# Expert biases: from bias products on TensorE to rows loaded to all partitions and added by VectorE

## The chip, the cores and the metric

The kernel runs on one core of a Trainium2 chip. The metric is the device time of one execution in microseconds (us). Five engines work side by side: TensorE (PE in the profile: matmuls; PEld: its weight loads), VectorE (DVE), ScalarE (ACT), GpSimd (POOL) and SyncE (SP), which here issues the loads. Each runs its own instructions in the order written and waits on semaphores. Sixteen DMA engines move the data.

## The reference

One inference step of a one-layer decoder for 512 prompt tokens and 64 sample tokens, model width 1024: two token mixers (gated linear attention and sparse attention), an output projection, and a mixture of experts, 4 of 32 per token. The change concerns the experts only. Each expert's tokens form a block of 128 rows, and for a block `xb` with expert `e` the reference computes

```python
gate = jnp.minimum(xb @ w_gate[e] + b_gate[e], SWIGLU_LIMIT)
up = jnp.clip(xb @ w_up[e] + b_up[e], -SWIGLU_LIMIT, SWIGLU_LIMIT)
return ((up + 1.0) * gate * jax.nn.sigmoid(SWIGLU_ALPHA * gate)) @ w_down[e] + b_down[e]
```

with `SWIGLU_LIMIT` 7 and `SWIGLU_ALPHA` 1.702. All three weight matrices of an expert are 1024 x 1024 in fp32. The rows that come out are weighed and added to their tokens. `b_down` enters elsewhere and isn't touched.

## The kernel before, in words

Seven stages follow each other, with a barrier between them. The last, `experts`, handles 32 blocks (one per expert here) and takes about two thirds of the time. A block needs three products of 128 x 1024 by 1024 x 1024: gate, up and down. Each weight matrix is loaded in four quarters of 1024 KB (two of the eight 128-row slices each), so a block has twelve quarters. `load_quarter` issues one on SyncE into one of six landing slots.

For accuracy in TensorE's faster fp32 form, both operands are split into a rounded high part and a rest. For a quarter, ScalarE writes the high part (`high_part`, L3064), VectorE the rest (`rest_part`, L3152: quarter minus high part). Both go to rings of four slots. TensorE then runs 12 matmuls of 512 columns for the quarter (`product`, L2950) and increments `s_used`. ScalarE may write a slot of the ring when the product four quarters earlier is done; SyncE may reload a landing slot when the rest of the quarter six earlier is written (`s_rest`).

The order of a step on each engine, written out by hand (`step`), for block k and its predecessor `prev`:

- TensorE: gate(k) with 4 quarters, the turn of the activations of k-1 (8 transposes, L2958), up(k), the turn of the input rows of k+1, down(k-1).
- VectorE: rests 4 to 6, `read_gate` (L3165: PSUM to `g`, min with 7), rest 7, the rest of the turned activations (`rest_T`, L3156), rests 8 to 10, `read_up` (L3171: PSUM to `u`, clipped), `activate` (L3176: (u+1)*g, L3179: times the sigmoid), rest 11, the rest of the turned rows (L3156), rests 0 to 3 of the next block.
- ScalarE: high parts 4 to 7, the sigmoid (L3081), the high part of the turned activations (`acts_T`, L3067), high parts 8 to 11, that of the turned rows, high parts 0 to 2, the weighing of the down product (L3095), high part 3.
- SyncE: bias rows of block k (L2831), then the loads of gate, up and down quarters.
- GpSimd: the gather of a block's input rows (L2193) and the scatter that adds a block's output rows in memory (L2911).

The biases enter the sums as products. In the router stage GpSimd splits `b_gate` and `b_up` into three bf16 parts (L2341 to L2344) and stores them (L2346); SyncE waits for that (`s_bp`) before it issues the first weight quarters. In a step SyncE loads, for each of gate and up and each half of 512 columns, three rows of 512 bf16 to partitions 0, 32, 64 and 96 onward (four loads of 3 KB). TensorE begins the sums of gate and up with four matmuls of 3 rows (`start_with_bias`, L2936) with `ones` as the other operand, all four ahead of gate(k).

## Time and profile before

| | us |
|---|---|
| median of 3 runs | 1809.06 |
| their range | 1807.79 to 1809.69 |
| the profiled execution's own time | 1809.45 |
| its span | 1807.3 |

| engine | busy us | share of the span |
|---|---|---|
| TensorE, matmuls | 1691.8 | 94% |
| VectorE | 1424.3 | 79% |
| ScalarE | 1103.0 | 61% |
| GpSimd | 330.7 | 18% |

The span runs from the first to the last instruction. Matmuls are pipelined and their ends modelled, so a busy TensorE is not one at its peak. A releaser ("<-") is what ended an engine's idle time. Shares over the whole span mix stages with different limits, so the rows below are mostly of the expert stage, which begins near 640 us.

### The profile page before, as it was taken

To read this page: it belongs to the slowest core of one execution; us is meant where nothing else is said; L and a number is where in the kernel's file an instruction comes from. 1 tells how busy PE (TensorE), PEld (TensorE's weight loads), DVE (VectorE), ACT (ScalarE), POOL (GpSimd) and SP (SyncE) were. 2 spreads that over 40 slices of the span, in tenths; PEclk is the share of its full clock that TensorE was granted. 3 is DMA by queue.
4 is the path that set the end of the run, shared out by engine and by line. 5 is a ranking of instruction groups with operands and counts; after the bars stand their busy time and mean duration, and the time that the engine had idled before them with its cause. 6 is when DMAs were issued, how large, how long until landed. Compare 5 with 4: busy or idle time off the path is not lost.

```text
span 1807.3 us, 27029 instructions
## 1 busy us (share of the span) xinstructions
PE 1691.8 (94%) x9028; PEld 1311.5 (73%) x9028; DVE 1424.3 (79%) x1356; ACT 1103.0 (61%) x1052; POOL 330.7 (18%) x310
## 2 busy tenths in 40 slices
PE   3999978888998779999999999999999999999996
PEld 2776766555564568888888888888888888888884
DVE  4422563577425879999999999999999999999997
ACT  4222343354334366777777777777777777777773
POOL 0000011300001012122222312222231222223211
PEclk9999999599998779999999999999999999999998
DMA  9454553610226479999999999999999999999993
GB/s 347 174 185 172 98 157 97 223 80 3 69 97 188 173 276 335 379 376 374 369 378 377 372 374 379 377 373 373 379 374 373 387 371 373 384 373 374 385 349 124
DMA packets 114598, 516.08 MB, mean 286 GB/s; under 512 B 25870, under 2 KB 47710, under 8 KB 62058
## 3 DMA queue, kind: packets, MB, share of 16 engines
q1 hardware_dynamic: 101082, 483.48, 70.9%
q0 software_dynamic: 12800, 29.45, 5.8%
q10 hardware_dynamic: 656, 2.36, 0.3%
q8 instruction: 36, 0.59, 0.1%
q14 instruction: 24, 0.20, 0.0%
HBM read 502.75 MB, written 31.09 MB: 295 GB/s over the span
## 4 chain that ended last, share of the span: by engine, by line
PE 61%; DVE 1%; DMA 1%; ACT 0%; issue 0%; SPq 0%; DVEq 0%; POOL 0%; POOLq 0%; ACTq 0%
PE banks L2950 57%; PE banks L2958 3%; PE banks L2936 1%; DMA routing<-in_g_final 0%; DMA ffn_rows<-weighed,block_rows 0%; DVE split L3152 0%; DVE arena L3249 0%; PE banks L3005 0%; ACT split L3064 0%; DVE arena L3242 0%; DVE arena L3241 0%; SPq L2870 0%; DVEq L2816 0%; POOL wait_taken L2888 0%; DVE gates L3165 0%
## 5 line engine op out<-in xcount | busy, mean ns | idle before, releaser
L2950 PE MATMUL banks<-split 128*128 128x512 f32 x4608 | 1076.9, 393 | 1.1 <-DVE split L3152 1.1
L2950 PEld LDWEIGHTS banks<-split 128*128 128x128 f32 x4608 | 861.0, 188 | 186.2 <-issue 7.2
L3152 DVE TENSOR_TENSOR split<-expert_buffers,split 128x2048 fp32r<-128x2048 f32 x384 | 864.8, 2284 | 42.7 <-ACT split L3064 40.5
L3064 ACT ACTIVATE split<-expert_buffers 128x2048 fp32r<-128x2048 f32 x384 | 733.2, 1918 | 217.1 <-PE banks L2950 213.3
L2888 POOL TENSOR_TENSOR wait_taken<-routing 128x1 f32<-128x1 f32 x62 | 76.3, 1231 | 811.7 <-PE banks L2958 464.6
L2911 POOL DMA_INDIRECT ffn_rows<-weighed,block_rows x31 | 107.7, 3473 | 4.8 <-issue 4.8
L662 PE MATMUL banks<-w_in_high,hT_high 128*128 128x476 f32 x192 | 76.0, 396 | 4.4 <-DVE hT_low L498 4.4
L3156 DVE TENSOR_TENSOR split<-banks,split 128x1024 fp32r<-128x1024 f32 x64 | 77.8, 1215 | 0.7 <-ACT split L3067 0.7
L662 PE MATMUL banks<-w_in_high,hT_low 128*128 128x476 f32 x192 | 73.5, 383 | 0.0
L3067 ACT ACTIVATE split<-banks 128x1024 fp32r<-128x1024 f32 x64 | 64.5, 1008 | 6.0 <-PE banks L2958 6.0
L573 DVE COPY arena<-banks 128x476 f32<-128x476 f32 x12 | 7.8, 654 | 70.0 <-PE banks L662 69.9
L662 PE MATMUL banks<-w_in_low,hT_high 128*128 128x476 f32 x160 | 60.5, 378 | 0.0
L1850 ACT ACTIVATE arena<-banks 128x512 f32<-128x512 f32 (+1 forms) x45 | 24.5, 586 | 58.1 <-PE banks L2114 19.3
L1520 ACT ACTIVATE arena<-banks,arena 128x128 f32<-128x128 f32 (+3 forms) x64 | 33.2, 526 | 39.2 <-DVE arena L1562 39.0
L662 PEld LDWEIGHTS banks<-w_in_high,hT_high 128*128 128x128 f32 x192 | 36.8, 192 | 22.0 <-issue 16.8
L3095 ACT ACTIVATE weighed<-banks,block_weights 128x1024 f32<-128x1024 f32 x31 | 34.6, 1117 | 29.3 <-PE banks L2950 29.3
L3081 ACT ACTIVATE sigmoids<-gates 128x1024 f32<-128x1024 f32 x32 | 34.0, 1063 | 26.2 <-DVE gates L3165 26.2
L2893 POOL TENSOR_TENSOR routing<-routing 128x1 int32<-128x1 int32 x31 | 40.6, 1310 | 16.1 <-issue 8.3
L840 POOL MEMSET arena<- 128x2560 f32 x1 | 2.2, 2237 | 214.2 <-POOLq L127 214.2
L662 PEld LDWEIGHTS banks<-w_in_high,hT_low 128*128 128x128 f32 x192 | 36.8, 191 | 5.8
L2958 PEld LDWEIGHTS banks<-routing 128*128 128x128 f32 x256 | 33.9, 192 | 9.1 <-DVE bias_ones L3147 6.7
L3179 DVE TENSOR_TENSOR ups<-ups,sigmoids 128x1024 f32<-128x1024 f32 x32 | 39.3, 1230 | 1.1
(396 smaller groups left out, 1728.5 us busy)
## 6 DMA issues: line engine op xcount, KB each, us to landing
expert_buffers<-in_w_gate SPq DMA_DIRECT2D x128, 1024.0 KB, 8.0
expert_buffers<-in_w_up SPq DMA_DIRECT2D x128, 1024.0 KB, 19.0
expert_buffers<-in_w_down SPq DMA_DIRECT2D x128, 1024.0 KB, 8.6
arena<-in_w_ada SPq DMA_DIRECT2D x16, 1024.0 KB, 4.9
w_in_landing<-in_w_in SPq DMA_DIRECT2D x5, 1904.0 KB, 9.0
arena<-in_w_ada SPq DMA_DIRECT2D x4, 2048.0 KB, 19.9
arena<-in_x_prompt SPq DMA_DIRECT2D x8, 512.0 KB, 9.4
arena<-in_cache_cmp SPq DMA_DIRECT2D x32, 128.0 KB, 2.9
```

What stands on the lines that cost most here:

```text
L662: last = pe.matmul(ps[0:n, 4 + t, 0:CW], h[:, kt, t0:t0 + n].bitcast(F32R), w.bitcast(F32R), start=(kt == 0 and j == 0), stop=(kt == KT - ...
L2888: pool.tensor_tensor(sums[s_sum.index(sem)], one, one, ALU.add).then_inc(sem, 1)
L2893: pool.tensor_tensor(tokens, core.row_of[:, bass.ds(k, 1)], none, ALU.add).then_inc(s_tok, 1)
L2911: pool.indirect_dma_start(core.ffn_d, bass.IndirectOffsetOnAxis(ap=row_out.bitcast(U32), axis=0), y, None, bounds_check=NTOK - 1, oob_is_e ...
L2950: last = pe.matmul(ps[:, bank + c, :], x[:, kt * P:(kt + 1) * P].bitcast(F32R), wt.bitcast(F32R), start=(m == 2 and kt == 0 and x is xs[0] ...
L2958: last = pe.transpose(ps[:, TB + kt // 4, (kt % 4) * P:(kt % 4 + 1) * P], v[:, kt, :], ident)
L3064: act.activation(high[:, j % RING_Q].bitcast(F32R), v, ACT.Copy).then_inc(s_high, 1)
L3067: act.activation(dst.bitcast(F32R), ps[:, TB:TB + 2, :].rearrange("p b n -> p (b n)"), ACT.Copy).then_inc(sem, 1)
L3095: act.activation(y, ps[:, DB:DB + 2, :].rearrange("p b n -> p (b n)"), ACT.Copy, scale=weight_out).then_inc(s_y, 1)
L3152: dve.tensor_tensor(rest[:, j % RING_Q].bitcast(F32R), v, high[:, j % RING_Q], ALU.subtract).then_inc(s_rest, 1)
L3156: dve.tensor_tensor(lo.bitcast(F32R), ps[:, TB:TB + 2, :].rearrange("p b n -> p (b n)"), hi, ALU.subtract).then_inc(out, 1)
L3179: dve.tensor_tensor(u, u, s, ALU.mult).then_inc(s_a, 1)
```

## The change

The bias parts, their store and their waits go from the router stage, and the bias matmuls from TensorE; the first matmul of each sum now starts it. SyncE loads the 4 KB bias row of the expert, once for gate and once for up, to all 128 partitions, straight into `g` and `u`: the gates' once the previous activation is done (`s_a`), between the first and second up quarters, and the ups' once the previous activations are turned (`s_atp`), behind the down quarters. VectorE adds as it reads, so the clipping is done afterwards. For the gates it is folded into the product with the sigmoid (`gated`, placed ahead of rest 10), while ScalarE takes relu(7 - g) first and then a sigmoid of 1.702 * 7 - 1.702 * that, which is the sigmoid of 1.702 * min(g, 7). For the ups it is an instruction of its own.

```diff
@@ router stage
-                    for i, name in enumerate(("b_gate", "b_up")):
-                        sp.dma_start(b32[:, i * BQ:(i + 1) * BQ], io[name][0].rearrange("e (q n) -> (e q) n", n=BQ)).then_inc(s_b, 16)
...
-                    sp.wait_ge(s_bp, 1)
...
-            pool.wait_ge(s_b, 32)
-            for a in range(3):
-                if a < 2:
-                    link(pool.tensor_copy(bparts[:, a, :], b32))
-                    link(pool.tensor_tensor(b32, b32, bparts[:, a, :], ALU.subtract))
-                else:
-                    pool.tensor_copy(bparts[:, a, :], b32).then_inc(s_bp, 1)
-            pool.wait_ge(s_bp, 1)
-            pool.dma_start(core.bias_d.rearrange("e q a m n -> (e q) (a m n)"), bparts.rearrange("p a n -> p (a n)")
-                           ).then_inc(s_bo, 16)
...
@@ experts, SyncE
+            def load_biases(m, e):
+
+                sp.dma_start((g, u)[m], core.io[("b_gate", "b_up")[m]][0][bass.ds(e, 1), :].to_broadcast([P, D])
+                             ).then_inc(s_bias[m], 16)
...
             e = expert(0)
-            biases(0, e, None)
-            biases(1, e, None)
-
             for q in range(2, 4):
                 sp.wait_ge(s_rest, q - 1)
                 load_quarter(core, sp, e, 1, q, q - 2)
+            sp.wait_ge(core.s_begun, 16 * ST)
+            for m in range(2):
+                load_biases(m, e)
 
             def step(k, prev):
 
-                free = 1 if is_zero(prev) else 12 * prev
                 e = expert(k)
-                biases(0, e, free)
-                biases(1, e, free)
                 quarters(0, e, prev, 0)
-                e = expert(k)
-                quarters(1, e, prev, 4)
-                e = expert(prev)
-                quarters(2, e, prev, 8)
+                quarters(1, e, prev, 4, range(1))
+                sp.wait_ge(s_a, k)
+                load_biases(0, e)
+                quarters(1, e, prev, 4, range(1, 4))
+                quarters(2, expert(prev), prev, 8)
+                sp.wait_ge(s_atp, k)
+                load_biases(1, e)
@@ experts, TensorE
-            def start_with_bias(m, n, bank):
-
-                pe.wait_ge(s_bias[m], 32 * n)
-                for c in range(2):
-                    r0 = bias_row(m, c)
-                    pe.matmul(ps[:, bank + c, :], ones[r0:r0 + 3, :], bias[r0:r0 + 3, :], start=True, stop=False)
-
...
-                                             start=(m == 2 and kt == 0 and x is xs[0] and wt is hi[c]),
+                                             start=(kt == 0 and x is xs[0] and wt is hi[c]),
...
-                start_with_bias(0, k + 1, GB)
-                start_with_bias(1, k + 1, UB)
...
@@ experts, ScalarE
                 if is_zero(k):
+                    act.wait_ge(s_seven, 1)
                     act.wait_ge(core.s_begun, 16 * ST)
-                act.activation(s, g, ACT.Sigmoid, scale=ALPHA).then_inc(s_sig, 1)
+                act.activation(s, g, ACT.Relu, scale=-1.0, bias=seven[:, 0:1]).then_inc(s_room, 1)
+                act.wait_ge(s_room, k + 1)
+                act.activation(s, s, ACT.Sigmoid, scale=-ALPHA, bias=seven[:, 1:2]).then_inc(s_sig, 1)
@@ experts, VectorE
-                else:
-                    dve.wait_ge(s_a, k)
-                dve.tensor_scalar(g, ps[:, GB:GB + 2, :].rearrange("p b n -> p (b n)"), LIMIT, None, ALU.min).then_inc(s_g, 1)
+                dve.wait_ge(s_bias[0], 16 * (k + 1))
+                dve.tensor_tensor(g, ps[:, GB:GB + 2, :].rearrange("p b n -> p (b n)"), g, ALU.add).then_inc(s_g, 1)
+
+            def gated(k):
+                dve.wait_ge(s_sig, k + 1)
+                dve.scalar_tensor_tensor(g, g, LIMIT, s, ALU.min, ALU.mult).then_inc(s_part, 1)
 
             def read_up(k, used):
                 dve.wait_ge(s_used, used)
-                if not is_zero(k):
-                    dve.wait_ge(s_atp, k)
-                dve.tensor_scalar(u, ps[:, UB:UB + 2, :].rearrange("p b n -> p (b n)"), -LIMIT, LIMIT, ALU.max, ALU.min
-                                  ).then_inc(s_u, 1)
+                dve.wait_ge(s_bias[1], 16 * (k + 1))
+                dve.tensor_tensor(u, ps[:, UB:UB + 2, :].rearrange("p b n -> p (b n)"), u, ALU.add).then_inc(s_u, 1)
 
             def activate(k):
                 dve.wait_ge(s_u, k + 1)
-                dve.scalar_tensor_tensor(u, u, 1.0, g, ALU.add, ALU.mult).then_inc(s_t, 1)
-                dve.wait_ge(s_t, k + 1)
-                dve.wait_ge(s_sig, k + 1)
-                dve.tensor_tensor(u, u, s, ALU.mult).then_inc(s_a, 1)
+                dve.tensor_scalar(u, u, -LIMIT, LIMIT, ALU.max, ALU.min).then_inc(s_clip, 1)
+                dve.wait_ge(s_clip, k + 1)
+                dve.wait_ge(s_part, k + 1)
+                dve.scalar_tensor_tensor(u, u, 1.0, g, ALU.add, ALU.mult).then_inc(s_a, 1)
...
-                for j in range(8, 11):
+                for j in range(8, 10):
                     rest_part(j, prev)
+                gated(k)
+                rest_part(10, prev)
                 read_up(k, at + 8)
                 activate(k)
                 rest_part(11, prev)
```

## Rows read from the trace of the kernel before

**Rows 1.** Chain that ended last, by line, from the page.
```profile
PE banks L2950 57%; PE banks L2958 3%; PE banks L2936 1%; DMA routing<-in_g_final 0%; DMA ffn_rows<-weighed,block_rows 0%; DVE split L3152 0%; DVE arena L3249 0%; PE banks L3005 0%; ACT split L3064 0%; DVE arena L3242 0%; DVE arena L3241 0%; SPq L2870 0%; DVEq L2816 0%; POOL wait_taken L2888 0%; DVE gates L3165 0%
```
**Rows 2.** Timeline of one step, VectorE and ScalarE (start us, us, instruction, [idle before]).
```profile
1007.35 1.22 DVE L3165 TENSOR_SCALAR gates<-banks 128x1024 f32<-128x1024 f32 x1
1008.48 2.28 DVE L3152 TENSOR_TENSOR split<-expert_buffers,split 128x2048 fp32r<-128x2048 f32 x1
1008.60 1.06 ACT L3081 ACTIVATE sigmoids<-gates 128x1024 f32<-128x1024 f32 x1 [0.77 <-DVE gates L3165]
1009.57 1.01 ACT L3067 ACTIVATE split<-banks 128x1024 fp32r<-128x1024 f32 x1
1010.47 3.75 ACT L3064 ACTIVATE split<-expert_buffers 128x2048 fp32r<-128x2048 f32 x2
1010.68 1.22 DVE L3156 TENSOR_TENSOR split<-banks,split 128x1024 fp32r<-128x1024 f32 x1
1012.40 6.85 DVE L3152 TENSOR_TENSOR split<-expert_buffers,split 128x2048 fp32r<-128x2048 f32 x3 [0.51 <-ACT split L3064]
...
1019.17 1.22 DVE L3171 TENSOR_SCALAR ups<-banks 128x1024 f32<-128x1024 f32 x1
...
1020.43 1.23 DVE L3176 SCALAR_TENSOR_TENSOR ups<-ups,gates 128x1024 f32<-128x1024 f32 x1
...
1021.69 1.23 DVE L3179 TENSOR_TENSOR ups<-ups,sigmoids 128x1024 f32<-128x1024 f32 x1
1022.84 2.28 DVE L3152 TENSOR_TENSOR split<-expert_buffers,split 128x2048 fp32r<-128x2048 f32 x1
...
1025.04 1.21 DVE L3156 TENSOR_TENSOR split<-banks,split 128x1024 fp32r<-128x1024 f32 x1
1026.18 11.08 DVE L3152 TENSOR_TENSOR split<-expert_buffers,split 128x2048 fp32r<-128x2048 f32 x5
...
1037.50 2.29 DVE L3152 TENSOR_TENSOR split<-expert_buffers,split 128x2048 fp32r<-128x2048 f32 x1 [0.24 <-ACT split L3064]
...
1040.23 2.29 DVE L3152 TENSOR_TENSOR split<-expert_buffers,split 128x2048 fp32r<-128x2048 f32 x1 [0.43 <-ACT split L3064]
...
1042.44 1.22 DVE L3165 TENSOR_SCALAR gates<-banks 128x1024 f32<-128x1024 f32 x1
```
**Rows 3.** Windows: length, busy us of each engine, PEclk, DMA share, GB/s.
```profile
1007.35:1042.44 35.09, 35.09 (x166) 28.85 (x165) 33.77 (x20) 26.75 (x17) 9.00 (x7) 1.00 0.98 371
...
970.00:975.00 5.00, 5.00 (x28) 4.25 (x27) 4.95 (x3) 3.42 (x4) 0.00 (x0) 1.00 1.02 347
975.00:980.00 5.00, 5.00 (x24) 4.14 (x23) 4.49 (x4) 4.20 (x4) 0.00 (x0) 1.00 1.01 415
```
**Rows 4.** Table of waits, 700 to 1750 us (total us, times, longest).
```profile
ACT split L3064 <- PE banks L2950: 199.2, 270, 0.8
DVE split L3152 <- ACT split L3064: 35.4, 90, 0.5
```
**Rows 5.** Timeline of TensorE where a step begins.
```profile
1029.41 0.40 PE L2936 MATMUL banks<-block_biases,bias_ones 3*128 3x512 bf16 x4
1029.74 11.22 PE L2950 MATMUL banks<-split 128*128 128x512 f32 x48
```
**Rows 6.** Groups by line and shape, VectorE, an earlier stage.
```profile
L456 DVE TENSOR_SCALAR arena<-arena 128x1024 f32<-128x1024 f32 x4 | 2.9, 746 | 10.0 <-ACT arena L358 10.0
```
**Rows 7.** One scatter (timeline); all scatters, 700 to 1750 us (median us to landing).
```profile
997.97 3.48 POOL L2911 DMA_INDIRECT ffn_rows<-weighed,block_rows  x1 [0.15 <-issue]
...
ffn_rows<-weighed,block_rows POOLq DMA_INDIRECT x30, 13.2
```
**Rows 8.** GpSimd's last bias pass (timeline); first weight loads (one line's instructions).
```profile
578.42 0.95 POOL L2344 CAST arena<-arena 128x512 bf16<-128x512 f32 x1
...
L2727 SPq DMA_DIRECT2D expert_buffers<-in_w_gate x4: 440/560/642, 614.4 to 616.0; - x4
```
**Rows 9.** One line's instructions, the sigmoid (duration ns, first and last start).
```profile
L3081 ACT ACT_TABLE_LOAD  x1: 1283/1283/1283, 658.7 to 658.7; - x1
```

More of the change, by code:

```diff
@@ L2250, in output_and_router @@
     upper = Stack(core, core.z1 + NT * D + ST * 512, ARENA)
-    BQ = D * NE // P
-    b32 = core.arena[:, hole[0]:hole[0] + 2 * BQ]
-    bparts = upper.take(3 * 2 * BQ // 2).bitcast(BF16).rearrange("p (a n) -> p a n", a=3)
     bsplit = core.named("down_bias_split", upper.at, D)[:, 0:D]
@@ L2763, in experts @@
     w, s_w = core.w, core.s_w
-    bias = own("block_biases", 512 // 2).bitcast(BF16)
-    ones = own("bias_ones", P // 2).bitcast(BF16)
+    seven = own("limit", 2)
     xg, tokens, none = core.xg, core.tokens, core.none
@@ L2773, in experts @@
     s_bias = [core.sem(f"bias_in{i}") for i in range(2)]
+    s_seven, s_part, s_room, s_clip = core.sem("limit_ready"), core.sem("gate_times_sigmoid"), core.sem("gate_room"), core.sem("up_clipped")
     s_high, s_rest, s_used = (core.sem(n) for n in ("quarters_rounded", "quarters_split", "quarters_used"))
     s_xg = core.s_xg
[L2776 to L2777 removed]
+    s_rowo, s_xtp, s_xh, s_xt = (core.sem(n) for n in (
+        "weights_taken", "xT_ps", "xT_rounded", "xT_split"))
     s_g, s_u, s_sig, s_a, s_atp, s_ah, s_at = (core.sem(n) for n in (
         "gate_read", "up_read", "sigmoid", "act_ready", "aT_ps", "aT_rounded", "aT_split"))
[L2780 removed]
+    s_y, s_yo = core.sem("down_read"), core.sem("rows_added")
     s_tok = core.sem("tokens_taken")
@@ L2823, in expert, with quarters @@
                 return sp.value_load(blocks[0:1, bass.ds(k, 1)], min_val=0, max_val=NE - 1)
-            def biases(m, e, used):
-                if used is not None:
-                    sp.wait_ge(s_used, used)
-                for c in range(2):
-                    r0 = bias_row(m, c)
-                    sp.dma_start(bias[r0:r0 + 3, :].rearrange("a (q n) -> a q n", q=2),
-                                 core.bias_d[bass.ds(e, 1), 2 * c:2 * c + 2, :, m, :].rearrange("e q a n -> (e a) q n")
-                                 ).then_inc(s_bias[m], 16)
-            def quarters(m, e, prev, c):
-                for q in range(4):
+            def load_biases(m, e):
+                sp.dma_start((g, u)[m], core.io[("b_gate", "b_up")[m]][0][bass.ds(e, 1), :].to_broadcast([P, D])
+                             ).then_inc(s_bias[m], 16)
+            def quarters(m, e, prev, c, some=range(4)):
+                for q in some:
                     sp.wait_ge(s_rest, 12 * prev + c + q + 9 - LANDING)
@@ L3146, in _ @@
         def _(dve):
-            dve.memset(ones, 1.0).then_inc(s_ones, 1)
+            dve.memset(seven[:, 0:1], LIMIT)
+            dve.memset(seven[:, 1:2], LIMIT * ALPHA).then_inc(s_seven, 1)
             def rest_part(j, prev):
```

22 lines of the change are left out of this document (6 added, 16 removed).

## The prediction, made before the result was known

> **What bounds the kernel now.** I read the page's chain of waits first: 57% of the span on it is the matmul line of the expert products, L2950, and the lines of VectorE and ScalarE have 0% each [rows 1]. The span holds 32 blocks of the expert stage, and in it each step is alike, so I read one step closely, from one read of the gates by VectorE (L3165, at 1007.35) to the next (1042.44): a step of 35.09 us [rows 2]. In that window TensorE is busy for all of it at the full clock, VectorE for 33.77 us, ScalarE for 26.75 us, and the DMA engines for a share of 0.98 at 371 GB/s [rows 3]. So three resources stand close together: TensorE sets the pace, VectorE has 1.3 us to spare, the DMA engines next to nothing by their share. The table of waits says how they hang together: ScalarE's rounding (L3064) waits for TensorE 270 times (199.2 us, ring of four slots), VectorE's subtraction (L3152) waits for ScalarE 90 times, 35.4 us in all, or 1.2 us a step [rows 4]. VectorE idles only because it has caught up with the ring. Its idle places are in [rows 2]: 0.51 us before rest 8 (at 1012.40), 0.24 and 0.43 us before rests 5 and 6 (1037.50 and 1040.23). ("Rest n" is the n-th L3152 of the written order of a step.)
>
> How late may VectorE be? Rest 0 of the next block ends at 1026.18 + 2.28 = 1028.46 [rows 2], the product that uses it starts at 1029.74 [rows 5]: 1.3 us. That is the tightest place; I take it as the slack.
>
> **TensorE's part.** Four bias matmuls go. They use rows 0, 32, 64 and 96, start within 0.1 us of each other and the next matmul starts 0.33 us after the first of them [rows 5]. 128 instructions of 384 ns would look like 49 us; they are worth 0.33 us x 32 = 10.6 us at most. TensorE's step would be 35.09 - 0.33 = 34.76 us. The waits on the gate and up reads stay, so the idle before them stays as well; if it went too, 0.3 us more a step would be saved, and if something of the bias time only turns into that idle, nothing. I take 34.76.
>
> **VectorE's part.** The two reads become additions of a PSUM and an SBUF operand. The same kind of instruction of the same size stands in the step: L3156, 1.21 us, against 1.22 us for the read [rows 2]. Nothing changes. Of the two instructions after read_up, one (min and product with the sigmoid) moves ahead of rest 10, one clip is added, one stays. Start to start, now: L3171 to L3176 1.26, L3176 to L3179 1.26, L3179 to rest 11 1.15, together 3.67 us [rows 2]. Then: read_up 1.26, clip, product 1.15. The clip is a one-input instruction from SBUF to SBUF. That kind, 128x1024 f32, took 746 ns [rows 6]; read from PSUM it takes 1.22 us [rows 2]. The source here is SBUF, so I take 0.75 + 0.03 = 0.78 us, and 1.26 as the upper end. Sum 3.19 us, plus 1.15 for the moved one: 4.34, so +0.67 us a step (up to +1.15).
>
> **ScalarE's part, and the detour.** Sigmoid becomes two passes, Relu and Sigmoid, each taken at the 1.06 us of the sigmoid row, and a wait for its own result between them (0.05 us, estimated from the 0.03 to 0.1 us between an end and a dependent start in [rows 2]). ScalarE has time for it on average (26.75 + 1.1 of 35 us). But behind the sigmoid in its fixed order stands the rounding of the turned activations (L3067), and behind that the rounding of quarter 8, and VectorE waits for both. Now: gates read until 1008.57, sigmoid 1008.60, L3067 1009.57, high part 8 from 1010.47 to 1012.39, rest 8 at 1012.40 [rows 2]; that chain is already the one that ends last, as the 0.51 us of idle shows. Rest 7 (to 1010.76) covers only the first part. With one more pass: Relu 1008.60 to 1009.66, sigmoid 1009.71, L3067 from 1010.68, high part 8 from 1011.58 to 1013.50, rest 8 at 1013.52. That is +1.12 us, and no work of VectorE's can fill it, since its order is fixed too. The ends: Relu as cheap as the cheapest pass of 1024 elements in the step, L3067 at 1.01 us, +1.06; with a slow hand-over, +1.25.
>
> **VectorE's step.** Packed, without the idle before rests 5 and 6, the step now is: read_gate to rest 8 5.05, to read_up 6.77, to rest 11 3.67, to rest 0 3.34, seven rests at (11.08 - 2.28) / 4 = 2.20 each 15.4; sum 34.23 us [rows 2]. New: 34.23 + 1.12 + 0.67 = 36.02 us. It begins and ends on VectorE, so slack can't absorb it for long, and it is above TensorE's 34.76. TensorE is then held at rests 11 and 0. The idle before rests 5 and 6 should go, since TensorE is no longer ahead.
>
> Per step 36.02 - 35.09 = +0.93 us. There are 31 steps with this order (blocks 1 to 31; in block 0 the placing of the overflow stands between the read and rest 7 and covers the longer sigmoid): +28.8 us, less the 1.3 us of slack used up once, less 0.3 us of bias matmuls in block 0: +27 us.
>
> **DMA.** A step loads twelve quarters of 1024 KB. The step moved 371 GB/s x 35.09 us = 13.0 MB [rows 3] (the quarters alone are 12.6). Each bias row of 4 KB is now written to 128 partitions: 2 x 128 x 4096 B = 1.05 MB a step; the old 3 KB loads were nothing. At 36.02 us that asks for (13.0 + 1.05) / 36.02 = 390 GB/s. Were these engines at their limit at a share of 0.98, they could give 371 / 0.98 = 379. But at full share they gave 347 in one stretch and 415 in the next of 5 us [rows 3]. The low stretch lies in the time of the adding scatter of the rows: it was issued at 997.97, so at 962.9 in the step before, and takes 13.2 us to land, until 976 [rows 7]. Taking 347 for 13.2 us and 414 for the rest, a step of 14.05 MB needs 13.2 + (14.05 - 4.58) / 0.414 = 36.1 us; by 379 throughout, 37.1 us. So this limit lies right beside VectorE's. As the load of the gates' bias stands in the queue ahead of two weight quarters whose slots were freed late (by rests 11 and 0; the second, freed at 1028.46, is wanted by ScalarE 1.92 us ahead of a rest 6 that, packed, would start 11.0 us later, so within 9.1 us), I add 0.2 us a step, between 0 and 0.5 (1.05 MB take 2.5 us of queue in all): +6 us.
>
> The Trainium skill's page "DMA: Bandwidth & Descriptors" (Specifications) has a limit of ~358 GB/s from HBM for a core; by it a step would take 14.05 / 0.358 = 39.2 us, some 1940 us in all, an estimate by that page of the Trainium skill. The trace already stands above that figure, 371 over a whole step and 415 at the best [rows 3], and the measurement decides; I give this nothing.
>
> **Waits that are added or moved.** SyncE waits for the activation (s_a) before the gates' bias, behind the first up quarter; the next quarter waits for rest 11, which follows the activation on VectorE, so nothing is late. It waits for s_atp before the ups' bias, at the place of the old bias loads, between rests 5 and 6; the next issue waits for rest 6. In the DMA-bound case it can be late. Landing has some 18 us for the gates and 14 for the ups: enough against 13.2 us, the longest landing in the rows [rows 7]. In the router stage GpSimd's five passes, a store, and SyncE's wait for them go. They end at 579.4, the first weight loads go out at 614.4 [rows 8]: nothing, and 1 us either way for what they disturbed.
>
> **Sum.** +27 + 6 = +33 us on the profiled execution's 1809.45 us (span 1807.3), which is 0.4 us above the median of the runs. Predicted: 1842 us.
>
> **Rivals.**
> DMA-bound, slower still: the bias writes don't fit, the six landing slots are all in flight, ScalarE waits for weights. 36.6 (the 36.1 with the waits of a full queue) to 37.4 us a step, 31 x 1.5 to 2.3 = +47 to +71: 1856 to 1880. For it: a share of 0.98 now. Against: no wait of ScalarE for a DMA in the table, and 415 GB/s beside the scatter.
> TensorE-bound, faster: the removed matmuls count and VectorE hides the rest. 31 x -0.33 = -10 us: 1799. It decides if VectorE's packed step stays below 34.76 us. VectorE's busy time alone would allow it (33.77 + 0.67 = 34.44); the detour behind the sigmoid, which already shows as idle, speaks against. If only half of both terms came, the step would be 35.1: no change, 1809.
> Relu and Sigmoid in different tables: two loads a step. The one load in [rows 9] took 1.28 us; both lie on the detour: +2.56 us a step, 79 us more: 1921. In this trace Sigmoid and Copy alternate after one load. "ScalarE: Activation LUTs" (Table sets) of the Trainium skill says that cheap functions such as relu are in every set; no row here has a Relu. I give it 2%.
>
> **How the numbers follow.** Forecast (chain of VectorE and ScalarE, 1834 to 1853): 57%. DMA-bound: 29%. Tables: 2%. TensorE-bound: 5%. No change: 3%. Forecast's mechanism with its lower ends (1825 to 1834): 4%. Range 1830 to 1880. A measurement of this kernel tells a change of about 0.2% (4 us) from none; so faster 5%, same 3%, slower 92%.
>
> **What would show it.** After: a step of 36 us; TensorE no longer busy for all of it, waiting for VectorE's L3152; VectorE idle for 1.0 us before the subtraction of the turned activations, waiting for ScalarE, and half a microsecond before rest 8; no idle at rests 5 and 6; the chain of waits running over VectorE and ScalarE; about 390 GB/s. ScalarE waiting for weights and steps over 36.6 us would speak for the DMA. A packed VectorE step under 35 us would make the prediction wrong, as would a clip at 1.2 us make it low.

## The result, and the profile after

The changed kernel takes 1845.61 us (median of 4 runs, 1843.81 to 1849.03) beside 1809.38 for the kernel before (4 runs): a ratio of 1.0197 with a 95% interval of [1.0183, 1.0212]. It is slower by 36 us; 1842 was predicted. The profiled execution took 1849.03 us (span 1846.9), 39.6 us more than the one before; it is the slowest of its four. One of the four executions of experiment e6 ran at a granted clock of 0.555 and took 2802.08 us; it is left out of that kernel's time.

The chain of waits by engine, from the page of the changed kernel. Before, 57% of it was TensorE's one matmul line [rows 1].

```profile
DVE 26%; issue 18%; DMA 10%; ACT 7%; PE 3%; DVEq 0%; SPq 0%; POOL 0%; ACTq 0%; POOLq 0%
```

The timeline of one step of VectorE and ScalarE, from one read of the gates (L3130) to the next. L3118 is the subtraction, L3122 the rest of something turned, L3026 the high part, L3029 the high part of something turned, L3134 `gated`, L3143 the clip.

```profile
1022.51 1.21 DVE L3130 TENSOR_TENSOR gates<-banks,gates 128x1024 f32<-128x1024 f32 x1
1023.65 2.28 DVE L3118 TENSOR_TENSOR split<-expert_buffers,split 128x2048 fp32r<-128x2048 f32 x1
1023.76 1.16 ACT L3044 ACTIVATE sigmoids<-gates,limit 128x1024 f32<-128x1024 f32 x1 [1.18 <-DVE gates L3130]
1024.95 1.15 ACT L3046 ACTIVATE sigmoids<-sigmoids,limit 128x1024 f32<-128x1024 f32 x1
1026.01 1.00 ACT L3029 ACTIVATE split<-banks 128x1024 fp32r<-128x1024 f32 x1
1026.91 7.49 ACT L3026 ACTIVATE split<-expert_buffers 128x2048 fp32r<-128x2048 f32 x4
1027.05 1.23 DVE L3122 TENSOR_TENSOR split<-banks,split 128x1024 fp32r<-128x1024 f32 x1 [1.12 <-ACT split L3029]
1028.85 4.49 DVE L3118 TENSOR_TENSOR split<-expert_buffers,split 128x2048 fp32r<-128x2048 f32 x2 [0.58 <-ACT split L3026]
1033.26 1.22 DVE L3134 SCALAR_TENSOR_TENSOR gates<-gates,sigmoids 128x1024 f32<-128x1024 f32 x1
...
1036.60 1.22 DVE L3139 TENSOR_TENSOR ups<-banks,ups 128x1024 f32<-128x1024 f32 x1
1037.85 0.69 DVE L3143 TENSOR_SCALAR ups<-ups 128x1024 f32<-128x1024 f32 x1
1038.58 1.23 DVE L3146 SCALAR_TENSOR_TENSOR ups<-ups,gates 128x1024 f32<-128x1024 f32 x1
...
1039.72 2.28 DVE L3118 TENSOR_TENSOR split<-expert_buffers,split 128x2048 fp32r<-128x2048 f32 x1
...
1043.06 15.49 DVE L3118 TENSOR_TENSOR split<-expert_buffers,split 128x2048 fp32r<-128x2048 f32 x7
...
1058.47 1.22 DVE L3130 TENSOR_TENSOR gates<-banks,gates 128x1024 f32<-128x1024 f32 x1
```

The detour shows here: behind the read of the gates VectorE has one subtraction, then it sits idle for 1.12 us until ScalarE has come through Relu, sigmoid and the turned activations, and for another 0.58 us until high part 8 is there. Before, the only idle here was 0.51 us [rows 2]. From 1043.06 seven rests run without a gap: VectorE no longer catches up with the ring.

Windows of that step, and of the 14 steps from the third read of the gates and the 14 behind them (us; busy us of PE, PEld, DVE, ACT, POOL; PEclk; DMA share; GB/s), then the waits from 700 to 1750 us:

```profile
1022.51:1058.47 35.96, 35.13 (x161) 28.66 (x160) 34.19 (x21) 27.81 (x18) 9.49 (x7) 1.00 1.00 390
734.88:1238.28 503.40, 491.98 (x2243) 401.74 (x2242) 478.82 (x267) 388.00 (x238) 132.60 (x98) 1.00 1.00 393
1238.28:1745.31 507.03, 491.73 (x2241) 401.36 (x2240) 479.98 (x267) 388.60 (x239) 135.36 (x99) 1.00 1.00 394
```

```profile
ACT split L3026 <- PE banks L2915: 73.4, 115, 0.9
ACT split L3026 <- DMA expert_buffers<-in_w_up: 60.3, 40, 2.7
...
ACT split L3026 <- DMA expert_buffers<-in_w_gate: 38.2, 48, 1.7
...
DVE split L3122 <- ACT split L3029: 28.7, 30, 1.1
```

The first 14 steps are 503.40 / 14 = 35.96 us each, the next 14 are 36.22. ScalarE's wait for TensorE has shrunk from 199.2 us to 73.4, and a wait that was not in the table before has come: ScalarE waits for weights.

Where the 39.6 us between the two profiled executions are:

| part | us |
|---|---|
| 30 steps from the second read of the gates on: 35.955 against 35.083 us | +26.2 |
| in the same steps, what they take beyond 35.955 us (0.6 of it in the first of them) | +4.4 |
| the first step (first to second read of the gates): 37.25 against 30.65 | +6.6 |
| behind the last read of the gates: 65.57 against 63.14 | +2.4 |
| ahead of the first read of the gates: 661.05 against 661.01 | 0.0 |

The first step in the timeline of the changed kernel, ScalarE, VectorE and SyncE's queue (SPq: start of the issue, time over which the group is issued):

```profile
661.05 1.22 DVE L3130 TENSOR_TENSOR gates<-banks,gates 128x1024 f32<-128x1024 f32 x1
661.16 0.33 SPq L2708 DMA_DIRECT2D expert_buffers<-in_w_up  x1
...
662.30 1.16 ACT L3044 ACTIVATE sigmoids<-gates,limit 128x1024 f32<-128x1024 f32 x1 [3.59 <-DVE gates L3130]
...
663.47 1.28 ACT L3046 ACT_TABLE_LOAD   x1
...
664.77 1.15 ACT L3046 ACTIVATE sigmoids<-sigmoids,limit 128x1024 f32<-128x1024 f32 x1
...
683.71 1.49 SPq L2708 DMA_DIRECT2D expert_buffers<-in_w_up  x3
...
690.02 1.92 ACT L3026 ACTIVATE split<-expert_buffers 128x2048 fp32r<-128x2048 f32 x1 [1.79 <-DMA expert_buffers<-in_w_up]
...
694.14 1.92 ACT L3026 ACTIVATE split<-expert_buffers 128x2048 fp32r<-128x2048 f32 x1 [2.21 <-DMA expert_buffers<-in_w_up]
```

Three things. The table load, which stood at 658.7 where ScalarE idled before the gates were read [rows 9], now stands between Relu and sigmoid.

Second, three up quarters of block 1 are issued only at 683.71, behind the wait for the first activation, which ends at 683.12. Before, the four went out from 661.27 on without that wait, the last three at 668.76, 670.96 and 677.23:

```profile
661.27 16.30 SPq L2727 DMA_DIRECT2D expert_buffers<-in_w_up  x4
```

In the changed kernel the slots of these three are free at 670.05, 672.25 and 680.12 (where the subtractions that read them end), so the wait holds them for 13.7, 11.9 and 4.5 us, and ScalarE waits for them.

Third, TensorE's clock. Windows of this step, first the changed kernel's, then one of the kernel before (busy us as above; the granted clock is the third number from the end):

```profile
671.00:674.00 3.00, 3.00 (x10) 2.35 (x9) 1.25 (x1) 0.32 (x1) 0.00 (x0) 0.59 0.00 0
678.00:682.00 4.00, 4.00 (x19) 3.77 (x19) 3.96 (x4) 2.26 (x2) 0.56 (x1) 0.55 0.26 73
682.00:686.00 4.00, 4.00 (x12) 3.17 (x11) 4.00 (x3) 0.00 (x0) 0.00 (x0) 0.60 0.38 114
```

```profile
678.00:682.00 4.00, 4.00 (x12) 3.13 (x11) 3.97 (x4) 0.00 (x0) 0.25 (x1) 0.57 0.73 262
```

A mean of 0.55 to 0.60 is a window spent mostly at the lower of the two levels (1.2 and 2.4 GHz). The changed kernel has two such stretches in its first step; the kernel before has one, and reads 1.00 over 671 to 674. Ahead of the first stretch TensorE had been idle for 2.54 us (to 670.10), before for 1.11 us (to 668.65). From 670.10 on, 12 matmuls take 4.27 us instead of 3.02, the 8 turns 1.44 instead of 1.05, and the 40 small matmuls of the overflow 6.04 instead of 4.67.

### The profile page after: what moved, and what is told of

It reads as the page before. It is cut to its first block, busy times and chain, and to the rows that moved or that the text cites. A ratio compares the mean times of both kernels' runs of the same rounds, so it can differ in the third digit from the quotient of the medians.

```text
span 1846.9 us, 26301 instructions
## 1 busy us (share of the span) xinstructions
PE 1693.7 (92%) x8900; PEld 1311.2 (71%) x8900; DVE 1438.9 (78%) x1389; ACT 1136.5 (62%) x1084; POOL 346.4 (19%) x304
## 4 chain that ended last, share of the span: by engine, by line
DVE 26%; issue 18%; DMA 10%; ACT 7%; PE 3%; DVEq 0%; SPq 0%; POOL 0%; ACTq 0%; POOLq 0%
DVE split L3118 18%; DMA expert_buffers<-in_w_up 8%; ACT split L3026 3%; PE banks L2915 3%; DVE split L3122 2%; DVE ups L3139 2%; ACT sigmoids L3044 2%; DMA expert_buffers<-in_w_down 2%; ACT split L3029 1%; DVE gates L3134 1%; DVE ups L3143 1%; DVE gates L3130 1%; DMA routing<-in_g_final 0%; DMA ffn_rows<-weighed,block_rows 0%; PE banks L2968 0%
## 5 line engine op out<-in xcount | busy, mean ns | idle before, releaser
L2915 PE MATMUL banks<-split 128*128 128x512 f32 x4608 | 1088.6, 394 | 35.9 <-DVE split L3118 32.3
L3118 DVE TENSOR_TENSOR split<-expert_buffers,split 128x2048 fp32r<-128x2048 f32 x384 | 859.6, 2284 | 34.1 <-ACT split L3026 33.9
L3026 ACT ACTIVATE split<-expert_buffers 128x2048 fp32r<-128x2048 f32 x384 | 728.6, 1915 | 203.7 <-PE banks L2915 86.9
L2860 POOL TENSOR_TENSOR wait_taken<-routing 128x1 f32<-128x1 f32 x62 | 63.3, 1020 | 836.0 <-PE banks L2923 490.2
L3122 DVE TENSOR_TENSOR split<-banks,split 128x1024 fp32r<-128x1024 f32 x64 | 78.1, 1221 | 30.9 <-ACT split L3029 30.9
L2193 POOL DMA_INDIRECT routing<-h_rows,routing x32 | 83.4, 2607 | 6.4 <-issue 1.7
L3029 ACT ACTIVATE split<-banks 128x1024 fp32r<-128x1024 f32 x64 | 64.4, 1006 | 7.7 <-PE banks L2923 7.6
L3044 ACT ACTIVATE sigmoids<-gates,limit 128x1024 f32<-128x1024 f32 x32 | 36.7, 1146 | 18.2 <-DVE gates L3130 18.2
```

The costliest lines, as they stand in the source:

```text
L2193: pool.indirect_dma_start(core.xg, None, core.h2_d, bass.IndirectOffsetOnAxis(ap=core.tokens.bitcast(U32), axis=0), bounds_check=NTOK - 1, ...
L2860: pool.tensor_tensor(sums[s_sum.index(sem)], one, one, ALU.add).then_inc(sem, 1)
L2915: last = pe.matmul(ps[:, bank + c, :], x[:, kt * P:(kt + 1) * P].bitcast(F32R), wt.bitcast(F32R), start=(kt == 0 and x is xs[0] and wt is ...
L3026: act.activation(high[:, j % RING_Q].bitcast(F32R), v, ACT.Copy).then_inc(s_high, 1)
L3029: act.activation(dst.bitcast(F32R), ps[:, TB:TB + 2, :].rearrange("p b n -> p (b n)"), ACT.Copy).then_inc(sem, 1)
L3044: act.activation(s, g, ACT.Relu, scale=-1.0, bias=seven[:, 0:1]).then_inc(s_room, 1)
```

## Experiments

All ratios are to the kernel before, timed on the same chip. "One pass" stands for this edit, which e1, e5, e9 and e10 share:

```diff
-                act.activation(s, g, ACT.Relu, scale=-1.0, bias=seven[:, 0:1]).then_inc(s_room, 1)
-                act.wait_ge(s_room, k + 1)
-                act.activation(s, s, ACT.Sigmoid, scale=-ALPHA, bias=seven[:, 1:2]).then_inc(s_sig, 1)
+                act.activation(s, g, ACT.Sigmoid, scale=ALPHA).then_inc(s_sig, 1)
```

**e1_one_pass.** The edit above alone.

> The changed kernel with one ScalarE pass again: the sigmoid reads the sum itself, without the Relu (it then sees sums over 7 unclipped; min with 7 is still taken in the product). My theory, the fixed-order chain of VectorE and ScalarE: the way from the gates' read to rest 8 shrinks by one pass of 1.15 us and its hand-over from 6.34 to about 5.1 us, VectorE's packed step from 35.95 to 34.7 us, TensorE's 34.76 takes over; with 2 us less in block 0, 1845.6 - 31 x 1.15 - 2 = 1808 us. Rival, the DMA engines: 14.05 MB in 34.8 us ask for 404 GB/s; if 390 is all they give, the step stays near 35.9 us and ScalarE waits for weights in place of the sigmoid: 1838 to 1844 us.

Measured 1839.50 us, 1.0174 [1.0148, 1.0199]: my theory was wrong, the rival right. The same 14 steps in windows, and two rows of its waits (700 to 1700 us):

```profile
725.22:1229.10 503.88, 491.17 (x2242) 401.41 (x2240) 480.34 (x267) 371.75 (x224) 127.25 (x98) 1.00 1.00 394
```

```profile
ACT split L3026 <- DMA expert_buffers<-in_w_up: 140.8, 89, 3.0
ACT split L3026 <- DMA expert_buffers<-in_w_gate: 79.4, 84, 1.7
```

The detour is gone, yet a step takes 503.88 / 14 = 35.99 us: the DMA engines, at 394 GB/s, hold the place that the chain has left.

**e2_rows16.** From block 1 on the bias row goes to 16 partitions, an eighth of the bytes (0.13 MB a step).

```diff
-            def load_biases(m, e):
-                sp.dma_start((g, u)[m], core.io[("b_gate", "b_up")[m]][0][bass.ds(e, 1), :].to_broadcast([P, D])
+            def load_biases(m, e, rows=16):
+                sp.dma_start((g, u)[m][0:rows, :], core.io[("b_gate", "b_up")[m]][0][bass.ds(e, 1), :].to_broadcast([rows, D])
...
-                load_biases(m, e)
+                load_biases(m, e, P)
```

> The changed kernel, but from block 1 on each bias row is loaded to 16 of the 128 partitions only (the other rows get stale values added), so a step moves 0.92 MB less, with every instruction and wait kept. Chain theory: the step stays at 35.95 us; only the steps with DMA waits (3.9 us in all) and part of the first step shorten: 1838 to 1842 us. DMA theory: the step falls by up to 0.9 us towards the step of before: 1815 to 1820 us.

Measured 1840.53 us, 1.0180 [1.0154, 1.0205]. No wait of ScalarE for a DMA is left, 29 of its last 30 steps are 35.95 to 35.97 us, and the queue moves less (the window is the changed kernel's):

```profile
734.88:1238.28 503.40, 491.62 (x2242) 401.36 (x2241) 478.66 (x267) 389.58 (x239) 133.04 (x98) 1.00 0.99 369
```

So the chain alone gives 35.95 us. Each limit alone costs nearly the whole: removing either gains 5 to 6 us in the median. In the profiles the first step (37.25 us in the changed kernel) is 34.27 in e2 and 32.67 in e1; the 30 steps behind it take 1083.0 us in the changed kernel, 1078.8 in e2 and 1079.6 in e1.

**e3_order.** The same work, with the turned activations and high part 8 ahead of the two passes.

```diff
-                sigmoid(k)
                 acts_T(k)
-                for j in range(8, 12):
+                high_part(8, prev)
+                sigmoid(k)
+                for j in range(9, 12):
```

> The changed kernel with ScalarE's order altered: rounding of the turned activations, high part 8, then Relu and sigmoid, then high part 9 (from block 1 on). Same work on every engine. Chain theory: VectorE's idle before the turned activations' rest (1.12) and before rest 8 (0.58) goes, its packed step is 35.95 - 1.70 = 34.25 us, TensorE's 34.76 bounds, 1845.6 - 31 x 1.15 = 1810 us. If VectorE's added work as such were the cost, or the DMA engines, nothing would change: 1840 to 1846 us.

Measured 1849.67 us, 1.0232 [1.0203, 1.0262]: missed by 40 us, and 4 us above the changed kernel. Its 14 steps take 36.2 us each, at nearly the rate of e1:

```profile
730.90:1237.35 506.45, 491.44 (x2241) 401.39 (x2240) 478.96 (x267) 386.43 (x239) 126.09 (x98) 1.00 1.00 393
```

**e6_order_rows16.** e3 with the 16-partition loads of e2.

> ScalarE's order altered (turned activations and high part 8 ahead of Relu and sigmoid) and the bias rows to 16 partitions from block 1 on. No pass and no VectorE instruction is taken away against the changed kernel. Two-limit theory: VectorE's packed step is 35.95 - 1.12 - 0.58 = 34.25 us, TensorE's step without products was 34.49 in the experiment on the kernel before and bounds: 1840.5 - 31 x 1.46 = 1795 us. If the added work on VectorE and ScalarE were what costs (0.7 and 1.3 us a step) rather than the place of the sigmoids in ScalarE's order: about 1840 us.

Measured 1835.92 us (3 runs), 1.0146 [1.0127, 1.0166]. Missed by 41 us. An early step shows why the order helps less than I thought:

```profile
771.20 3.70 ACT L3026 ACTIVATE split<-expert_buffers 128x2048 fp32r<-128x2048 f32 x2
773.13 2.29 DVE L3119 TENSOR_TENSOR split<-expert_buffers,split 128x2048 fp32r<-128x2048 f32 x1 [1.04 <-ACT split L3026]
```

The wait of 1.04 us now stands before rest 9: two passes (2.3 us) between high parts 8 and 9 are longer than what VectorE has between them. The detour was moved, not removed: this step is 35.21 us (765.34 to 800.55), not the 34.49 expected. From the eighth step on it is 35.5 to 36.3 us, at 371 GB/s, and ScalarE waits for weights: 66.9 us in all from 700 to 1750 us. The 16-partition loads didn't take these waits away here, as they did in e2.

**e4_before_no_products.** The kernel before without its bias matmuls, with the bias loads and all waits kept.

```diff
-                                             start=(m == 2 and kt == 0 and x is xs[0] and wt is hi[c]),
+                                             start=(kt == 0 and x is xs[0] and wt is hi[c]),
...
-                start_with_bias(0, k + 1, GB)
-                start_with_bias(1, k + 1, UB)
+                for m in range(2):
+                    pe.wait_ge(s_bias[m], 32 * (k + 1))
```

> The kernel before without the four bias matmuls of a step (the gate and up biases are left out of the result); bias loads and the waits for them stay. My price: TensorE's step 35.09 - 0.33 = 34.76 us, 31 steps: 1809.4 - 10.5 = 1799 us. By the instructions' listed durations (384 ns each) it would be 49 us less, 1760; if the idle for waits at the start of a step merely fills the gap, 1809.

Measured 1788.86 us, 0.9891 [0.9857, 0.9925]. Every step from the third on is 34.48 to 34.50 us. The products cost 35.09 - 34.49 = 0.60 us a step, nearly twice the 0.33 that I had read between their start and the next matmul's [rows 5]. The rest lies in the junctions around them: in this kernel the down and the gate product run on as one group of 96 matmuls, 1011.61 to 1033.48, 10.93 us for 48; before, 48 matmuls from 1018.34 to the bias products at 1029.41 took 11.07, and the 48 behind them, from 1029.74 to 1040.80, 11.06. Twice 0.13 to 0.14 us is the missing 0.27.

**e5_one_pass_rows16.** One pass and the 16-partition loads.

> One ScalarE pass (no Relu) and the bias rows to 16 partitions from block 1 on, both in one kernel (biases of the other rows stale, sums over 7 unclipped in the sigmoid). Each alone left the step at 36.0 us. My theory now: two limits lie side by side, the chain of VectorE and ScalarE (35.95 us) and the DMA engines (14.05 MB at about 391 GB/s, 36.0 us), and each hid the gain of taking the other away. With both gone the packed step of VectorE is 35.95 - 1.24 = 34.7 us: 1840.5 - 31 x 1.25 - 2 = 1800 us. Rival: neither the bias bytes nor the detour is the cost, but VectorE's added clip and the new waits: the step stays at 35.5 to 36, 1828 to 1841 us.

Measured 1827.31 us, 1.0104 [1.0087, 1.012]. Its second to fourth steps were 34.87, 34.70 and 34.68 us, as the theory of two limits has it; then they drifted up, to 35.3 to 36.3 from the eighth on, with ScalarE waiting for weights at a rate far below 394:

```profile
1229.58:1730.55 500.97, 490.82 (x2242) 401.45 (x2240) 480.15 (x268) 373.13 (x224) 129.52 (x99) 1.00 0.99 373
```

**e7_twice.** The changed kernel with each bias row loaded a second time, to unused space, from block 2 on: 1.05 MB more a step.

```diff
+                if not is_zero(prev):
+                    sp.dma_start(f[:, 1, :], core.io["b_up"][0][bass.ds(e, 1), :].to_broadcast([P, D])).then_inc(s_spare[1], 16)
```

(and the same for `b_gate`).

> The changed kernel with each bias row of blocks 2 to 31 loaded a second time, to space that is unused then, at the same places: 1.05 MB more a step, 15.1 MB. If the DMA engines are at their limit at 391 to 395 GB/s: 15.1 / 0.393 = 38.4 us a step, +2.4 on 30 steps, 1845.6 + 73 = 1918 us. If they had room for more (415 GB/s as in the best stretches of before): 36.4 us, 1860 us.

Measured 1923.86 us, 1.0636 [1.062, 1.0653]:

```profile
734.58:1277.66 543.08, 504.09 (x2251) 407.37 (x2250) 482.44 (x268) 385.99 (x239) 151.93 (x98) 0.99 1.01 395
```

543.08 / 14 = 38.79 us a step at 395 GB/s. Against e1's 35.99 that is 2.8 us for 1.05 MB, 375 GB/s at the margin. Three kernels with different work (e1, e3, e7) and the second half of the changed one all run at 392 to 395 GB/s: this is what this mix of transfers got here over hundreds of microseconds.

**e9_spread_one_pass.** A way out of the bytes: SyncE loads the bias row to one partition, GpSimd spreads it to all. With one pass, e3's order, and all four up quarters of block 1 ahead of the wait for the activation.

```diff
+            def spread(m, k):
+                pool.wait_ge(s_bias[m], 16 * (k + 1))
...
+                pool.partition_broadcast((g, u)[m], (g, u)[m][0:1, :]).then_inc(s_spread[m], 1)
```

> A version meant to be better than both: the bias row is loaded to one partition and spread by GpSimd's partition broadcast; one ScalarE pass (the sigmoid of sums over 7 differs from that of 7 by under 7e-6, and the product still takes the minimum); ScalarE rounds the turned activations and high part 8 ahead of the sigmoid; in the step of block 1 SyncE waits for the activation only behind all four up quarters. No bias matmuls, 0.008 MB of biases a step. Two-limit theory: both limits are out of the way, TensorE's 34.49 us bounds; 31 x -0.60 and nothing lost at the start: 1789 to 1795 us. If GpSimd's spread comes late (it follows a scatter) or slows VectorE at a shared port, 1800 to 1840 us.

Measured 2287.94 us, 1.265 [1.2632, 1.2668]. GpSimd's timeline:

```profile
1001.50 2.18 POOL L2894 TENSOR_TENSOR bias_taken<-routing 128x1 f32<-128x1 f32 x1
1013.31 1.30 POOL L2895 PARTITION_BROADCAST gates<-gates  x1 [9.62 <-issue]
1022.15 1.51 POOL L2894 TENSOR_TENSOR bias_taken<-routing 128x1 f32<-128x1 f32 x1 [7.54 <-issue]
1031.80 1.30 POOL L2895 PARTITION_BROADCAST ups<-ups  x1 [8.15 <-issue]
1039.82 2.18 POOL L2869 TENSOR_TENSOR routing<-routing 128x1 int32<-128x1 int32 x1 [6.71 <-issue]
```

The broadcast is 1.30 us, but each comes with 8 to 10 us of idle before it and some 7 to 8 us behind it, mostly put down to no wait ("issue"). Two a step fill the engine. The trace has a candidate: an operation named MODIFY_POOL_CONFIG, which the timeline doesn't list, on GpSimd's queue. For the 64 broadcasts:

```profile
L2895 POOLq MODIFY_POOL_CONFIG  x128: 1/2/9, 655.0 to 2225.2; - x128
```

Two stand at 1003.9, where the idle before the broadcast of 1013.31 begins, and two more at 1033.0, behind that of 1031.80. The changed kernel has two in its whole trace. That they are the cost wasn't tested.

**e10_one_pass_no_loads.** The clean form of e5: one pass, and no bias load after block 0.

```diff
-                sp.wait_ge(s_a, k)
-                load_biases(0, e)
...
-                sp.wait_ge(s_atp, k)
-                load_biases(1, e)
...
-                dve.wait_ge(s_bias[0], 16 * (k + 1))
+                if is_zero(k):
+                    dve.wait_ge(s_bias[0], 16)
+                else:
+                    dve.wait_ge(s_a, k)
```

> The changed kernel with one pass (sigmoid of the unclipped sum) and with no bias rows loaded after those of block 0; both reads still add, whatever stands in the tile. Left out: the clip ahead of the sigmoid, and the right biases from block 1 on. Theory of two limits side by side (VectorE's and ScalarE's fixed order at 35.95 us, the DMA engines at 36.0 us for 14.05 MB): with both gone the step is VectorE's 34.23 + 0.67 = 34.9 us or, as the first steps of e5 showed, 34.7, throughout: some 1800 to 1806 us. Rival: what slowed the later steps of e5 (35.4 to 36.2) was not the bias bytes but something that a busy chain does to the weight loads: then it stays near 35.5 us a step, 1825 to 1830 us.

Measured 1796.76 us, 0.9934 [0.9916, 0.9951]. All steps behind the first are 34.68 or 34.69 us, 1040.5 us for the 30, and none of ScalarE's waits from 700 us on is for a DMA:

```profile
1210.47:1696.04 485.57, 485.57 (x2241) 402.47 (x2240) 477.48 (x267) 372.20 (x225) 122.72 (x99) 1.00 0.99 381
```

Removing both limits gives 49 us; removing one gave 5 (e2) and 6 (e1). And e5 differs from it by two loads of 64 KB a step and SyncE's two waits ahead of them, and is 31 us slower. The waits hold next to nothing back: from block 4 on eleven of twelve weight loads of e5 go out within 0.17 us of the end of the rest that frees their slot, as in e10, and the first gate quarter after 0.48 us (0.17 in e10). So a load of few bytes to few partitions isn't a load that is gone. The Trainium skill's page "SBUF — State Buffer" (Door 1: The DMA port swizzle) says that partitions 0 to 15 reach 4 of the 16 ports that transfers go through. These runs fit that, but none varies the partitions alone, and in e2, at 35.96 us a step, the same loads brought no wait; so the cause isn't shown.

**e11_before_two_passes.** The kernel before, bias products and all, with ScalarE's second pass alone (the "one pass" diff turned round, and the constants for it).

> The kernel before, with bias products and all, and only ScalarE's second pass added (Relu of 7 - g, then the sigmoid of that; same values). The path over ScalarE: VectorE's packed step 34.23 + 1.25 = 35.5 us against 35.09, so +0.4 us x 31 = +12, and +2.5 in the first step for the table load between the passes: 1821 to 1825 us. Rival: TensorE goes on setting the pace and covers the pass, since ScalarE is busy for 26.75 of 35 us: 1809 us (the first step's 2.5 us at the most).

Measured 1821.80 us, 1.0068 [1.0049, 1.0086]. The theory holds. The steps are 35.36 us (35.09 before), the first 32.41 (30.65). The wait is the changed kernel's:

```profile
DVE split L3163 <- ACT split L3069: 32.5, 29, 1.1
```

So the pass alone takes the pace away from TensorE, though ScalarE is busy for less than 80 of 100 us.

**e12_first_steps.** The changed kernel with two edits to its first steps.

```diff
-                quarters(1, e, prev, 4, range(1))
+                now = 4 if is_zero(prev) else 1
+                quarters(1, e, prev, 4, range(now))
...
-                quarters(1, e, prev, 4, range(1, 4))
+                quarters(1, e, prev, 4, range(now, 4))
...
+            act.wait_ge(s_seven, 1)
+            act.activation(early, seven[:, 0:1], ACT.Sigmoid)
             sigmoid(0)
```

> The changed kernel with two edits for the first steps alone: SyncE issues all four up quarters of block 1 before it waits for the activation of block 0, and a one-column sigmoid ahead of the first Relu has the table loaded while ScalarE idles. Theory: the first step (37.25 us against 30.65 before) owes 2.6 us to the table load and some 4 us to the held loads: 1838.5 to 1840.5 us. Rival: the first steps are held by the longer chain itself: under 2 us gained, 1844 to 1846 us.

Measured 1843.22 us (5 runs, 1839.96 to 1844.74), 1.0180 [1.0165, 1.0196]. The first step is 30.13 us instead of 37.25, all 7 us of it, and the granted clock is 1.00 in every window of it. Only 2.4 us of them reach the median, and the two intervals overlap: the first half of the steps, at the chain's 35.96 us in the changed kernel, now takes 36.12 each, and the second 36.30 (36.22), 3.3 us over the 30 steps.

```profile
1232.38:1740.61 508.23, 491.61 (x2242) 401.38 (x2241) 480.06 (x268) 388.32 (x239) 131.20 (x99) 1.00 1.01 393
```

I read this as the DMA engines holding the place that the chain has left, as in e1. The two edits together remove the first step's loss; what each is worth wasn't run. The total came out between theory and rival.

**e13_products_at_end.** The kernel before with its four bias products moved from the start of the gate product to its end, ahead of the turn of the activations. Nothing is left out.

```diff
+                    if m == 0 and q == 3 and end is not None:
+                        last = bias_products(end)
...
-                start_with_bias(0, k + 1, GB)
-                start_with_bias(1, k + 1, UB)
-                product(0, (xh, xl), GB, before)
+                product(0, (xh, xl), GB, before, end=k + 1)
```

> The kernel before with its bias products moved from the start of the gate product to its end, next to the turn of the activations; same values. Without the products a step was 34.49 us against 35.09: 0.33 us of products and 0.27 around them. Theory: the 0.27 us is the change of matmul form in the middle of a run of 128-row matmuls, and a turn has such a break anyway, so a part is saved: 0.1 to 0.2 us a step, 1803 to 1806 us. Rival: the products and their waits cost the same wherever they stand, or delay the read of the gates by 0.33 us which sits on the chain of VectorE: 1809 us or a little more.

Measured 1803.13 us (8 runs, 1802.42 to 1806.08) beside 1809.80 (13 runs, 1805.83 to 1812.61), 0.9970 [0.9959, 0.998]: 0.3% faster than the kernel before. TensorE's timeline:

```profile
1014.99 22.02 PE L2952 MATMUL banks<-split 128*128 128x512 f32 x96
1036.94 0.40 PE L2937 MATMUL banks<-block_biases,bias_ones 3*128 3x512 bf16 x4
1037.27 1.15 PE L2962 MATMUL banks<-routing,ups 128*128 128x128 f32 x8
```

Down and gate run as one group again. A step is 35.00 us, so 31 steps explain 2.8 of the 6.7 us; as much again lies ahead of the first read of the gates (658.27 against 661.01), where the traces of these kernels differ among each other by several us (657.6 in e1, 667.2 in e5). That part stays open.

## Why the prediction was right, and where it wasn't

**The step.** The forecast's mechanism was the right one: the chain over VectorE and ScalarE sets the pace, with 36.02 us predicted and 35.96 measured, throughout the first half of the stage; in the second half the DMA engines add 0.3 us. By its terms, predicted and measured [rows 2 before]:

| stretch | predicted | measured |
|---|---|---|
| read of the gates to rest 8 | 6.17 | 6.34 |
| rest 8 to read of the ups, with `gated` | 7.92 | 7.75 |
| read of the ups to rest 11 | 3.19 | 3.12 |
| rest 11 to rest 0 | 3.34 | 3.34 |
| seven rests | 15.4 | 15.41 |

The passes are 1.16 and 1.15 us, not 1.06: both have a bias column, and the sigmoid without one is 1.06 [rows 2] and 1.04 in e1. The clip took 0.69 us; the row of an earlier stage (0.75) [rows 6] was the right one of the two ends. The 7.92 still held 0.17 us that VectorE spent waiting for the ups before; that went. The two idles came where they were said to come, 1.12 and 0.58 us for 1.0 and 0.5.

e11 and e10 split the change. ScalarE's pass alone, in the old kernel, costs 35.36 - 35.09 = 0.27 us a step: read of the gates to rest 8 is 6.33 us there instead of 5.05, and 1.0 of these 1.28 us had stood elsewhere in the step as waits of VectorE's (35.09 - 34.23 = 0.86, and the 0.17 before the ups). VectorE's moved and added work without the pass and without the loads ends at 34.68, below the 35.09 of before: alone, with TensorE's products gone, it would have let the TensorE-bound rival come out, even a little better than its 1799 us (e10: 1796.8). The prediction gave as its condition a packed step under 34.76; that holds in e10.

**TensorE's part** was mis-sized: 0.33 us a step where the products cost 0.60 (e4). It changed nothing in the sum, as TensorE waits in the changed kernel. "If it went too, 0.3 us more" stood there as the other end, and that end was the true one.

**DMA.** The 0.2 us a step added for the queue (+6) came out as 4.4 us over the 30 steps, 0.6 of it in the first of them. "This limit lies right beside VectorE's" was right: 36.1 us by the split rates, and 35.99 in e1. The other figure, 379 GB/s from 371 and a share of 0.98, was wrong as a ceiling: the engines gave 394. The share reads 0.99 at 369 GB/s (e2) and 1.00 at 394: it doesn't say how much is left. The limit of ~358 GB/s that I had quoted from the Trainium skill ("DMA: Bandwidth & Descriptors", Specifications) is passed here by 10% over 500 us at a stretch with all transfers counted (393), and by 2% with the weights alone (twelve quarters of 1024 KB in e4's 34.49 us, 365 GB/s).

**What failed.** The first step, priced at nothing, cost 6.6 us. "Nothing is late" was said of SyncE's wait for the activation, worked out for a step of the loop. In block 1 it isn't so: there the activation of block 0 ends at 683.1, three loads stand behind it for 4.5 to 13.7 us, and ScalarE waits for them for 1.8, 2.2 and 0.4 us. And "block 0 covers the longer sigmoid" held for most of the pass but not for the table load, of which I had asked only whether there would be more of them, not where the one would stand. The clock was in no term at all. Counted from the read of the gates, the changed kernel is 1.4 us late when the 12 matmuls begin (9.05 us for 7.64): the pass and the load, as far as they aren't covered. It is 4.1 us late when the gate product begins (20.36 for 16.30), with 3.0 us more for TensorE's matmuls at the lower clock and 0.33 less for the products that are gone. The last 2.5 us come with ScalarE's waits for the held loads. e12, where the first step falls back to 30.13 us, shows that the load and the held quarters are behind it; it doesn't separate them. In e2, with the same table load and the same held quarters but an eighth of the bias bytes ahead of them, the step is 34.27 us, so these bytes have a share too. Whether the lower clock is in every execution isn't shown.

**Luck in the total.** The sum had 33 us, and the profiled execution took 39.6 more. The chain has 26.2 in the 30 steps (the sum 31 x 0.93 less 1.6, so about 26 for these), the queue 4.4 for 6, the first step 6.6 for nothing, and the part behind the last read of the gates 2.4, of which the sum had one step's 0.9. That 1842 lies within 0.2% of the median is in part because the median is 3.4 us below the profiled execution.

**GpSimd's passes** in the router stage are gone and the first read of the gates stands where it was (661.05 for 661.01): nothing, as said, as far as one trace tells; among the kernels with the changed router stage it stands between 657.6 and 667.2.

**The DMA-bound rival** (1856 to 1880) was mis-sized, not absent: its mechanism runs in the second half of the stage, at 36.2 us a step instead of 36.6 and more. Asking which of the two is the one bound of the changed kernel leads nowhere: e1 and e2 each take one away and both find the other at 36 us.

## What to carry to other kernels

Before removing a limit, work out the next one: two limits within 0.1 us of each other gave 5 and 6 us when removed one by one and 49 us together, and the time of neither single experiment would have told so. On an engine with a fixed order, ask what stands behind the longer instruction, not how busy the engine is: ScalarE idled a fifth of the time and its extra microsecond still set the pace. And work out the first steps of a loop by themselves: a wait that is harmless in the steady state held three loads for 5 to 14 us in the first, and a one-off table load moved onto the path.

## What the runs showed of the hardware

- Four bias products that run side by side in 0.33 us cost 0.60 us in the middle of a row of full matmuls, and 0.51 next to a turn (35.00 us a step in e13, 34.49 in e4).
- 392 to 395 GB/s of mixed loads over hundreds of microseconds, in e1, e3, e7, e12 and the changed kernel, with gate and down quarters landing in 11 to 13 us instead of 8 to 9 before (medians).
- Two loads of 64 KB to 16 partitions went with a slower stream for the others: 373 GB/s with ScalarE waiting (e5) and 371 (e6), where e5's kernel without them had no such wait at 381 (e10). At 369 GB/s they brought no wait (e2).
- GpSimd's partition broadcast is 1.30 us for 128 x 1024, with 7 to 10 us of idle on either side of it where it alternates with other work, and a MODIFY_POOL_CONFIG on the queue at each change (e9).
- Behind an idle of 2.54 us TensorE's granted clock was 0.59 over 671 to 674 us, and 12 matmuls took 4.27 us that take 3.02 at a clock of 1.00 (changed kernel and kernel before).
- Relu didn't need a table load of its own: in the loop Relu, Sigmoid and Copy alternate with none. But the one load stood between the first Relu and the first sigmoid, not ahead of both (663.47 us); a one-column sigmoid ahead of both had it at 658.27, in ScalarE's idle time (e12).
